# Rotary keys moved into the page rows of a paged latent cache, and split out again by GpSimd

## The chip, the cores and the metric

One core of one Trainium2 chip. The metric is device time in microseconds of one execution. PE is TensorE, PEld its weight loads, DVE is VectorE, ACT is ScalarE, POOL is GpSimd, SP is SyncE. All data is float32 unless said otherwise.

## The reference: what is computed

One layer of a decoder trunk for 512 prompt tokens and 8 sample tokens (one token each for 8 sequences), 520 rows of width 1024. An input projection makes query and key/value latents, a rotary key, a convolution input and two gates. Branch A is a gated depthwise convolution of width 31. Branch B is multi-head latent attention. Then come an output projection, a layer norm, a mixture of 32 experts (two per token) and a gated embedding.

The part at stake is the attention of the 8 sample tokens over a paged cache: 32 pages of 128 past tokens for each of the 8 sequences, 256 pages in all.

```
ckv_past = cache_ckv[layer, page_table]      # (8, 4096, 256)
kr_past  = cache_krope[layer, page_table]    # (8, 4096, 32)
s = (q_lat . ckv_past + q_rope . kr_past) * scale
p = softmax(s);  o = p . ckv_past
```

Every page thus has latents (256 numbers per token) that are used for the scores and again as values, and rotary keys (32 numbers per token) that are used for the scores alone.

## The kernel before, in words

The kernel is one hand-ordered program per engine. Semaphores join them; every instruction's place in its engine's stream is fixed.

**Stage 1** (0 to about 325 us) runs the input projection, the convolution and the gates in `UNITS` (`unit`, `paired`: lines 1019, 1059, 1068 and their neighbours) on PE. Between the units, at places worked out from matmul counts (`K_AT`, `T_AT`, `V_AT`), PE runs the paged attention in 16 steps of 16 pages. For step n there are three pieces: `k_step(n)` makes scores (line 1127: 32 matmuls with the latents; line 1131: 16 with the rotary keys), `k_turn(n)` transposes the probabilities (line 1143), and `v_step(n)` multiplies with the values (line 1157). On PE the order is k_step(0), k_turn(0), v_step(0), k_step(1), and so on, with unit matmuls between all of them.

**Pages.** A page is one DMA of 128 rows of 2048 bytes (`REC` = 512 numbers: two transposed latent chunks of 128, then 256 values) from `in_kv`, and one DMA of 32 rows of 512 bytes from `in_kr`. There are two buffers, chosen by n % 2. SP issues 10 of a step's 16 pages, POOL 6, each with its own semaphores (`s_kv`, `s_kvp`). Page j of a step has b, u = divmod(j, 4); its rotary keys go to partitions 32u to 32u+31 of `krr`, so the four pages of a group b lie below one another on the 128 partitions.

**Order on SP and POOL.** Both run the same loop. `step_keys(n)` loads the page numbers and issues the key DMAs, `step_pages(n)` loads the page numbers and issues the page DMAs:

```
for n in range(2, STEPS):
    pool.wait_ge(s_ks, n - 1)     # k_step(n-2) is done: key buffer free
    step_keys(n)
    pool.wait_ge(s_vs, n - 1)     # v_step(n-2) is done: page buffer free
    step_pages(n)
```

SP has the same, and before step 8 also the four stores of lines 773 to 777. Before `k_step(n)` PE waits for the semaphores of the step's pages and keys. POOL's other work in this stage is four copies of the prompt's rotary keys at its end (line 3015). DVE's stream (`steps`, `some_taps`) has, for each step, the maximum over the scores (`peaks`, line 2125, waits for `k_step(n)`), and between the units the taps of the convolution (line 2118), in order.

**Stages 2 and 3** (from 325 us) are the prompt's attention, the output projections, and the experts with their weight loads (`in_wexp`). The start of each of their transfers hangs on work of PE ahead of it.

Of the kernel before, what the change touches and what calls it, by code (L numbers as in the profile page):

```python
# [33 lines left out]
NPOOL = 5 * NS * NPAGES // 4  # L34
REC = 2 * P + KVL

# [242 lines left out]
A_UKT = A_WUQ + KQ * 2048  # L279
A_KR = A_KV + 2 * STEPS * REC  # L280
A_END1 = A_KR + 2 * 4 * P
assert A_QR + P <= A_OT and A_W1R + 4 * 1024 <= A_XT and A_UKT + 2048 <= A_END1

# [80 lines left out]
def decoder_layer(nc, a, o):  # L364

    ctx = ExitStack()
    with ctx:
# [9 lines left out]
        def at(off, n):  # L377
            return arena[:, off:off + n]
# [42 lines left out]
        kvr = at(A_KV, 2 * STEPS * REC).rearrange("p (s b u n) -> p s b u n", s=2, b=4, u=4)  # L421
        krr = at(A_KR, 2 * 4 * P).rearrange("p (s b n) -> p s b n", s=2, b=4)
        prb = at(A_P, 512).rearrange("p (s n) -> p s n", s=2)
# [281 lines left out]

        def page_keys(n, j):

            b, u = divmod(j, 4)
            return krr[32 * u:32 * u + 32, n % 2, b]

        def narrow(bank, rows, w, ready=None):
# [23 lines left out]
        def _(sp):  # L735
# [21 lines left out]

            def step_keys(n):
                sp.load(numbers, pages[0:1, STEPS * n:STEPS * n + SPN])
                for j in range(SPN):  # L760
                    pg = sp.snap(numbers[j], min_val=0, max_val=NPOOL - 1)
                    sp.dma_start(page_keys(n, j), a["kr"][bass.ds(pg, 1)].rearrange("a p n -> (a p) n")).then_inc(s_kv[n % 2], 16)

            sp.wait_ge(s_con, 112)
            step_pages(0)
            step_keys(0)
            step_keys(1)
            sp.wait_ge(s_q4, 1)
            step_pages(1)
            for n in range(2, STEPS):  # L770
                if n == 8:
                    sp.wait_ge(s_gl, 2 * KC)
                    sp.dma_start(o["conv_p"], ext[:, :, NPR:NPR + CW - 1]).then_inc(s_out, 16)
                    sp.dma_start(o["conv_s"], exs[:]).then_inc(s_out, 16)
                    sp.wait_ge(s_nrm, N_NRM)
                    sp.dma_start(o["ckv"], hT[:, B_CKV:B_CKV + KKV, :]).then_inc(s_out, 16)
                    sp.dma_start(o["krope"], hT[64:96, B_KR, :]).then_inc(s_out, 16)
                sp.wait_ge(s_ks, n - 1)
                step_keys(n)
                sp.wait_ge(s_vs, n - 1)  # L780
                step_pages(n)
# [187 lines left out]
        def _(pe):  # L969
# [145 lines left out]
            def k_step(n):  # L1115
                s, r = n % 2, n // 8
                if n == 0:
                    pe.wait_ge(s_qd, 9)
                elif n >= 2:
                    pe.wait_ge(s_ep, n - 1)  # L1120
                pe.wait_ge(s_kv[s], 32 * SPN * (n // 2 + 1))
                pe.wait_ge(s_kvp[s], 32 * (STEPS - SPN) * (n // 2 + 1))
                bank = 4 + s
                for c in range(KKV):
                    for x in range(SIDES):
                        for bb in range(4):
                            mm(ps[32 * bb:32 * bb + 32, bank, 0:2 * P], qlat[:, c, x, 4 * r + bb, :],  # L1127
                               kvr[:, s, bb, 2 * x:2 * x + 2, c * P:(c + 1) * P], start=(c == 0 and x == 0), stop=False)
                for j in range(2):
                    for bb in range(4):  # L1130
                        y = mm(ps[32 * bb:32 * bb + 32, bank, j * P:(j + 1) * P], qrz[:, j, 4 * r + bb, :], krr[:, s, bb],
                               start=False, stop=(j == 1))
                y.then_inc(s_ks, 1)
# [12 lines left out]
            def v_step(n):  # L1146
                s = n % 2
                pe.wait_ge(s_td2, n + 1)
                if n == 0:
                    pe.wait_ge(s_qa, 3)  # L1150
                    pe.wait_ge(s_qd, 1)
                else:
                    pe.wait_ge(s_oa, n)
                for x in range(SIDES):
                    for u in range(2):
                        for bb in range(4):
                            y = mm(ps[32 * bb:32 * bb + 32, 7, x * KVL:(x + 1) * KVL], pts[:, s, u * P + 32 * bb:u * P + 32 * bb + 32],  # L1157
                                   kvr[:, s, bb, 2 * x + u, 2 * P:REC], start=(u == 0), stop=(u == 1))
                y.then_inc(s_vs, 1)
# [67 lines left out]
            def scores(p, s, x):  # L1227
                hh = 2 * p + x
                if x == 0:
                    pe.wait_ge(s_nout, 2 * p + 2)  # L1230
                    pe.wait_ge(s_kout, 2 * p + 2)
                pe.wait_ge(s_rout, 2 * hh + 2)
                if hh == 0:
                    pe.wait_ge(s_kf, 4)
                    pe.wait_ge(s_cse, 1)
                    pe.wait_ge(s_new, 7)
                else:
                    pe.wait_ge(s_mx, 4 * hh)
                for bank, tiles in ((2, (0, 2)), (3, (1,)), (4, (3,))):
                    for i in tiles:  # L1240
                        c0 = P if i == 2 else 0
                        y = mm(ps[:, bank, c0:c0 + (i + 1) * P], qT[:, p % 4, x, i * P:(i + 1) * P],  # L1242
                               kT[:, s, x, 0:(i + 1) * P], start=True, stop=True)
                    y.then_inc(s_s, 1)
# [1735 lines left out]
        def _(pool):  # L2980
# [11 lines left out]
            def step_keys(n):  # L2992
                pool.load(numbers, pages[0:1, STEPS * n + SPN:STEPS * (n + 1)])
                for j in range(STEPS - SPN):
                    pg = pool.snap(numbers[j], min_val=0, max_val=NPOOL - 1)
                    pool.dma_start(page_keys(n, SPN + j), a["kr"][bass.ds(pg, 1)].rearrange("a p n -> (a p) n")  # L2996
                                   ).then_inc(s_kvp[n % 2], 16)

            pool.wait_ge(s_con, 112)
            step_pages(0)  # L3000
            step_keys(0)
            step_keys(1)
            pool.wait_ge(s_q4, 1)
            step_pages(1)
            for n in range(2, STEPS):
                pool.wait_ge(s_ks, n - 1)
                step_keys(n)
                pool.wait_ge(s_vs, n - 1)
                step_pages(n)

            pool.wait_ge(s_vs, STEPS - 1)
# [128 lines left out]
def laid_out(i):  # L3140
# [19 lines left out]
    def by_pair(w):  # L3160
# [19 lines left out]
    ckT = ckv.transpose(0, 2, 1).reshape(NPOOL, KKV, P, PAGE).transpose(0, 2, 1, 3).reshape(NPOOL, P, KKV * PAGE)  # L3180
    krT = ckr.transpose(0, 2, 1)
    steps = i["page_table"].reshape(2, 4, NPAGES // 4, 4).transpose(0, 2, 1, 3)
# [5 lines left out]
        "w_plg": chunks(i["w_ple_gate"][0]), "w_plp": chunks(i["w_ple_proj"][0]), "plT": chunks(ple.T),  # L3188
        "kv": np.concatenate([ckT, ckv], 2), "kr": krT,
        "state": state, "vec": vec, "con": con, "rope": rope,  # L3190
# [28 lines left out]
```

## Time and profile before

| | us |
|---|---|
| median of 3 runs (range) | 935.86 (932.34 to 937.1) |
| the profiled execution, device time | 934.52 |
| the profiled execution, span of the trace | 932.8 |

Granted TensorE clock 0.99 on average. Read the profile as follows: busy time of each engine first, then the same by stretches of time, then what PE waited for in the stretch with the paged steps, and last the timelines of PE, POOL, SP and DVE around single steps. "issue" as a releaser means that the profile shows nothing that was waited for. Starts are us from the span's start.

### The profile page before, as it was taken

What the parts mean: (1) busy time and instruction counts of PE and PEld (TensorE: products, weight loads), DVE (VectorE), ACT (ScalarE), POOL (GpSimd) and SP (SyncE); (2) the same over time, 40 slices, a digit from 0 to 9 for tenths busy, and PEclk for the clock granted to TensorE, in tenths of its full rate; (3) what the DMA queues carried; (4) which work ended last, traced back from release to release, by engine and by line L of the source; (5) the groups of instructions that cost most, each with busy time, mean ns of one, the idle gap of its engine ahead of it and who ended that gap; (6) DMA issues with size and microseconds to landing.
All of it is one profiled execution on the core that took longest, in us unless ns stands there. A gap on an engine that the chain in (4) does not pass through costs nothing.

```text
span 932.8 us, 14793 instructions
## 1 busy us (share of the span) xinstructions
PE 886.6 (95%) x5217; PEld 533.3 (57%) x5217; DVE 482.7 (52%) x1093; ACT 247.0 (26%) x553; POOL 146.0 (16%) x242
## 2 busy tenths in 40 slices
PE   8999999999999999999999999899999889888897
PEld 7777777777776766656678644443333333333343
DVE  2343789977752258677666346661111211114784
ACT  1122221112243125756620111221111111002246
POOL 0323433334334000000000000011211101111000
PEclk9999999999999999999999999999999989989999
DMA  9977998999999420101241595639999999998601
GB/s 373 372 254 247 337 340 279 332 369 309 320 333 329 169 75 20 49 20 43 113 191 47 212 427 242 237 120 407 425 421 423 424 420 426 422 418 343 236 24 69
DMA packets 76178, 247.61 MB, mean 265 GB/s; under 512 B 15397, under 2 KB 22830, under 8 KB 67110
## 3 DMA queue, kind: packets, MB, share of 16 engines
q1 hardware_dynamic: 54422, 191.42, 53.4%
q0 software_dynamic: 16288, 35.29, 10.6%
q10 hardware_dynamic: 5392, 19.93, 6.0%
q8 instruction: 43, 0.70, 0.3%
q14 instruction: 33, 0.27, 0.1%
HBM read 240.98 MB, written 18.05 MB: 278 GB/s over the span
## 4 chain that ended last, share of the span: by engine, by line
PE 78%; DMA 12%; DVE 5%; issue 2%; ACT 2%; SPq 0%; POOL 0%; DVEq 0%; ACTq 0%; POOLq 0%
PE ps L1068 12%; PE ps L1572 9%; PE ps L1019 8%; DMA arena<-in_wexp 8%; PE ps L1492 6%; PE ps L1594 4%; PE ps L1416 4%; PE ps L1127 3%; PE ps L1157 3%; PE ps L1242 3%; PE ps L1059 3%; PE ps L1697 2%; PE ps L1264 2%; DMA y_scratch<-arena,idy 2%; PE ps L1206 2%
## 5 line engine op out<-in xcount | busy, mean ns | idle before, releaser
L1068 PE MATMUL ps<-arena 128*128 128x260 f32 x544 | 125.9, 387 | 1.4 <-DMA arena<-in_xT 0.9
L1068 PEld LDWEIGHTS ps<-arena 128*128 128x128 f32 x544 | 101.8, 191 | 22.4 <-issue 4.5
L2118 DVE SCALAR_TENSOR_TENSOR arena<-arena,vec 128x512 f32<-128x512 f32 x120 | 81.8, 745 | 0.0
L1019 PE MATMUL ps<-arena 128*128 128x260 f32 x336 | 78.5, 387 | 0.1
L1572 PE MATMUL ps<-arena 128*64 128x512 f32 x288 | 66.8, 617 | 7.4 <-DMA arena<-in_wexp 6.4
L2989 POOL DMA_DIRECT2D arena<-in_kv x96 | 52.3, 546 | 134.7 <-issue 130.9
L2814 DVE TENSOR_TENSOR arena<-ps,arena 128x256 f32<-128x256 f32 x18 | 7.6, 425 | 126.9 <-ACT arena L1967 126.9
L1594 PE MATMUL ps<-arena 128*64 128x512 f32 x288 | 67.4, 610 | 4.2 <-DMA arena<-in_wexp 4.2
L1019 PEld LDWEIGHTS ps<-arena 128*128 128x128 f32 x336 | 62.1, 190 | 12.9 <-issue 3.2
L1572 PE MATMUL ps<-arena,con 128*64 128x512 f32 x288 | 63.8, 595 | 2.3 <-DMA arena<-in_wexp 2.3
L2996 POOL DMA_DIRECT2D arena<-in_kr x96 | 48.2, 502 | 63.8 <-issue 57.2
L1492 PE MATMUL ps<-arena 128*128 128x512 f32 x128 | 58.0, 600 | 0.0
L1594 PEld LDWEIGHTS ps<-arena 128*64 128x64 f32 x288 | 22.1, 141 | 46.6 <-issue 46.6
L1572 PEld LDWEIGHTS ps<-arena 128*64 128x64 f32 x288 | 22.1, 142 | 45.9 <-issue 45.9
L1697 PE MATMUL ps<-arena 128*128 128x512 f32 x96 | 42.5, 596 | 3.0 <-DMA arena<-in_w_plg 1.7
L3042 POOL DMA_INDIRECT y_scratch<-arena,idy x18 | 18.6, 1032 | 171.0 <-PE ps L1557 121.1
L3021 POOL MEMSET peak<- 128x3 f32 x1 | 0.1, 101 | 276.4 <-PE ps L1492 276.4
L1572 PEld LDWEIGHTS ps<-arena,con 128*64 128x64 f32 x288 | 20.3, 137 | 39.4 <-issue 39.4
L1967 ACT ACTIVATE arena<-ps 128x256 f32<-128x256 f32 x18 | 6.9, 385 | 131.1 <-PE ps L1572 131.1
L1242 PE MATMUL ps<-arena 128*128 128x128 f32 (+3 forms) x128 | 38.0, 440 | 0.8 <-DVE arena L2384 0.8
L1127 PE MATMUL ps<-arena 128*32 128x256 f32 x512 | 30.9, 382 | 7.5 <-issue 7.5
L2824 DVE COPY arena<-ps 128x512 f32<-128x512 f32 x17 | 11.8, 692 | 50.8 <-PE ps L1594 50.8
(424 smaller groups left out, 1356.4 us busy)
## 6 DMA issues: line engine op xcount, KB each, us to landing
arena<-in_wexp SPq DMA_DIRECT2D x26, 2048.0 KB, 24.0
arena<-in_kv SPq DMA_DIRECT2D x160, 256.0 KB, 8.8
arena<-in_wexp SPq DMA_DIRECT2D x36, 1024.0 KB, 27.2
arena<-in_kv POOLq DMA_DIRECT2D x96, 256.0 KB, 7.3
arena<-in_w ACTq DMA_DIRECT2D x35, 512.0 KB, 8.4
arena<-in_wexp SPq DMA_DIRECT2D x16, 512.0 KB, 4.7
arena<-in_wo SPq DMA_DIRECT2D x8, 512.0 KB, 4.6
arena<-in_w_out SPq DMA_DIRECT2D x4, 1024.0 KB, 7.3
```

The source lines that it names most:

```text
L1019: y = mm(ps[:, paired_bank(p, n), 0:TH], left(k), right(k), start=(k == 0), stop=(k == KD // 2 - 1))
L1068: y = mm(ps[:, b + h, 0:TH], w[:, k], xT[:, k, h * TH:(h + 1) * TH], start=(k == 0), stop=(k == KD - 1))
L1127: mm(ps[32 * bb:32 * bb + 32, bank, 0:2 * P], qlat[:, c, x, 4 * r + bb, :], kvr[:, s, bb, 2 * x:2 * x + 2, c * P:(c + 1) * P], start=(c == ...
L1242: y = mm(ps[:, bank, c0:c0 + (i + 1) * P], qT[:, p % 4, x, i * P:(i + 1) * P], kT[:, s, x, 0:(i + 1) * P], start=True, stop=True)
L1416: y = mm(ps[:, bank, 0:TH], left(k), right(k), start=(k == 0), stop=(k == KD // 2 - 1))
L1492: y = mm(ps[:, b + h, :], mixT[:, k, t * P:(t + 1) * P], wbig[:, k, h * 512:(h + 1) * 512], start=(k == 0), stop=(k == KD - 1))
L1572: y = mm(ps[64 * x:64 * x + 64, 2, :], turned[:, k, 64 * x:64 * x + 64], wx[slot][:, x, k * 512:(k + 1) * 512], start=(k == 0), stop=(k == ...
L1594: y = mm(ps[64 * x:64 * x + 64, 6 + h, :], htT[:, c, 64 * x:64 * x + 64], wx[slot][:, x, o0:o0 + 512], start=(c == 0), stop=(c == 1))
L1697: y = mm(ps[:, b + h, :], fbT[:, u % 2, k], plg[k][:, h * 512:(h + 1) * 512], start=(k == 0), stop=(k == KD - 1))
L2118: y = v.scalar_tensor_tensor(out=aT[:, c, 0:NPR], in0=win, scalar=wt, in1=aT[:, c, 0:NPR], op0=ALU.mult, op1=ALU.add)
L2989: pool.dma_start(rec[:, n % 2, SPN + j], a["kv"][bass.ds(pg, 1)].rearrange("a p n -> (a p) n")).then_inc(s_kvp[n % 2], 16)
L2996: pool.dma_start(page_keys(n, SPN + j), a["kr"][bass.ds(pg, 1)].rearrange("a p n -> (a p) n")).then_inc(s_kvp[n % 2], 16)
```

## The change

The cache is laid out on the host with the rotary keys inside each page row: 2176 bytes per row (256 latent numbers, 32 key numbers, 256 values). The 128 x 32 keys of a page, which were 32 rows of 128 tokens, now fill 128 partitions: partition 32q + r holds component r of the tokens 32q to 32q+31. The tensor `in_kr` and all its DMAs are gone. POOL's `step_keys(n)` is now four copies of 64 partitions by 256 numbers each (4 groups, 2 pages, 32 tokens), two of which move from the lower half of the partitions to the upper or back; PE waits for them (`s_kf`) ahead of the rotary matmuls of `k_step(n)`. Those write their 128 columns in four runs of 32. The DMA scratch of 4096 bytes per partition makes room for `krr`, which is a tensor of its own now.

```diff
@@ -32,7 +32,7 @@
 ROPEW = KQ * P
 PAGE, NPAGES = 128, 32
 NPOOL = 5 * NS * NPAGES // 4
-REC = 2 * P + KVL
+REC = 2 * P + P // 4 + KVL
 
 
 SIDES, HH = 2, 16
@@ -277,8 +277,7 @@
 A_KV = A_PTS + 1024
 A_WUQ = A_KV + STEPS * REC
 A_UKT = A_WUQ + KQ * 2048
-A_KR = A_KV + 2 * STEPS * REC
-A_END1 = A_KR + 2 * 4 * P
+A_END1 = A_KV + 2 * STEPS * REC
 assert A_QR + P <= A_OT and A_W1R + 4 * 1024 <= A_XT and A_UKT + 2048 <= A_END1
 
 A_PAIR = A_XT
@@ -419,7 +418,7 @@
 
         rec = at(A_KV, 2 * STEPS * REC).rearrange("p (s j n) -> p s j n", s=2, j=STEPS)
         kvr = at(A_KV, 2 * STEPS * REC).rearrange("p (s b u n) -> p s b u n", s=2, b=4, u=4)
-        krr = at(A_KR, 2 * 4 * P).rearrange("p (s b n) -> p s b n", s=2, b=4)
+        krr = sb("krr", [P, 2 * 4 * P])[:].rearrange("p (s b u h i) -> p s b u h i", s=2, b=4, u=2, h=2)
         prb = at(A_P, 512).rearrange("p (s n) -> p s n", s=2)
         pts = at(A_PTS, 512).rearrange("p (s n) -> p s n", s=2)
         swap = at(A_SWAP, P)
@@ -703,11 +702,6 @@
 
         OV_SLOT, OV_LOADS = 0, sum(k % 3 == 0 for k in range(EPAIRS))
 
-        def page_keys(n, j):
-
-            b, u = divmod(j, 4)
-            return krr[32 * u:32 * u + 32, n % 2, b]
-
         def narrow(bank, rows, w, ready=None):
 
 
@@ -755,16 +749,8 @@
                     sp.dma_start(rec[:, n % 2, j], a["kv"][bass.ds(pg, 1)].rearrange("a p n -> (a p) n")
                                  ).then_inc(s_kv[n % 2], 16)
 
-            def step_keys(n):
-                sp.load(numbers, pages[0:1, STEPS * n:STEPS * n + SPN])
-                for j in range(SPN):
-                    pg = sp.snap(numbers[j], min_val=0, max_val=NPOOL - 1)
-                    sp.dma_start(page_keys(n, j), a["kr"][bass.ds(pg, 1)].rearrange("a p n -> (a p) n")).then_inc(s_kv[n % 2], 16)
-
             sp.wait_ge(s_con, 112)
             step_pages(0)
-            step_keys(0)
-            step_keys(1)
             sp.wait_ge(s_q4, 1)
             step_pages(1)
             for n in range(2, STEPS):
@@ -775,8 +761,6 @@
                     sp.wait_ge(s_nrm, N_NRM)
                     sp.dma_start(o["ckv"], hT[:, B_CKV:B_CKV + KKV, :]).then_inc(s_out, 16)
                     sp.dma_start(o["krope"], hT[64:96, B_KR, :]).then_inc(s_out, 16)
-                sp.wait_ge(s_ks, n - 1)
-                step_keys(n)
                 sp.wait_ge(s_vs, n - 1)
                 step_pages(n)
             sp.wait_ge(s_pu, PU[AT["ga", 7]])
@@ -1118,18 +1102,19 @@
                     pe.wait_ge(s_qd, 9)
                 elif n >= 2:
                     pe.wait_ge(s_ep, n - 1)
-                pe.wait_ge(s_kv[s], 32 * SPN * (n // 2 + 1))
-                pe.wait_ge(s_kvp[s], 32 * (STEPS - SPN) * (n // 2 + 1))
+                pe.wait_ge(s_kv[s], 16 * SPN * (n // 2 + 1))
+                pe.wait_ge(s_kvp[s], 16 * (STEPS - SPN) * (n // 2 + 1))
                 bank = 4 + s
                 for c in range(KKV):
                     for x in range(SIDES):
                         for bb in range(4):
                             mm(ps[32 * bb:32 * bb + 32, bank, 0:2 * P], qlat[:, c, x, 4 * r + bb, :],
                                kvr[:, s, bb, 2 * x:2 * x + 2, c * P:(c + 1) * P], start=(c == 0 and x == 0), stop=False)
+                pe.wait_ge(s_kf, 4 * (n + 1))
                 for j in range(2):
                     for bb in range(4):
-                        y = mm(ps[32 * bb:32 * bb + 32, bank, j * P:(j + 1) * P], qrz[:, j, 4 * r + bb, :], krr[:, s, bb],
-                               start=False, stop=(j == 1))
+                        y = mm(ps[32 * bb:32 * bb + 32, bank, 0:2 * P].rearrange("p (u h j i) -> p j u h i", u=2, h=2, j=2)[:, j],
+                               qrz[:, j, 4 * r + bb, :], krr[:, s, bb], start=False, stop=(j == 1))
                 y.then_inc(s_ks, 1)
 
             def k_turn(n):
@@ -1155,7 +1140,7 @@
                     for u in range(2):
                         for bb in range(4):
                             y = mm(ps[32 * bb:32 * bb + 32, 7, x * KVL:(x + 1) * KVL], pts[:, s, u * P + 32 * bb:u * P + 32 * bb + 32],
-                                   kvr[:, s, bb, 2 * x + u, 2 * P:REC], start=(u == 0), stop=(u == 1))
+                                   kvr[:, s, bb, 2 * x + u, 2 * P + 32:REC], start=(u == 0), stop=(u == 1))
                 y.then_inc(s_vs, 1)
 
 
@@ -1231,7 +1216,7 @@
                     pe.wait_ge(s_kout, 2 * p + 2)
                 pe.wait_ge(s_rout, 2 * hh + 2)
                 if hh == 0:
-                    pe.wait_ge(s_kf, 4)
+                    pe.wait_ge(s_kf, 4 * STEPS + 4)
                     pe.wait_ge(s_cse, 1)
                     pe.wait_ge(s_new, 7)
                 else:
@@ -2990,23 +2975,24 @@
                                    ).then_inc(s_kvp[n % 2], 16)
 
             def step_keys(n):
-                pool.load(numbers, pages[0:1, STEPS * n + SPN:STEPS * (n + 1)])
-                for j in range(STEPS - SPN):
-                    pg = pool.snap(numbers[j], min_val=0, max_val=NPOOL - 1)
-                    pool.dma_start(page_keys(n, SPN + j), a["kr"][bass.ds(pg, 1)].rearrange("a p n -> (a p) n")
-                                   ).then_inc(s_kvp[n % 2], 16)
+
+                pool.wait_ge(s_kv[n % 2], 16 * SPN * (n // 2 + 1))
+                pool.wait_ge(s_kvp[n % 2], 16 * (STEPS - SPN) * (n // 2 + 1))
+                for x in range(SIDES):
+                    for h in range(2):
+                        gp.tensor_copy(krr[64 * x:64 * x + 64, n % 2, :, :, h],
+                                       kvr[64 * h:64 * h + 64, n % 2, :, 2 * x:2 * x + 2, 2 * P:2 * P + 32]).then_inc(s_kf, 1)
 
             pool.wait_ge(s_con, 112)
             step_pages(0)
-            step_keys(0)
-            step_keys(1)
             pool.wait_ge(s_q4, 1)
             step_pages(1)
             for n in range(2, STEPS):
-                pool.wait_ge(s_ks, n - 1)
-                step_keys(n)
+                step_keys(n - 2)
                 pool.wait_ge(s_vs, n - 1)
                 step_pages(n)
+            for n in range(STEPS - 2, STEPS):
+                step_keys(n)
 
             pool.wait_ge(s_vs, STEPS - 1)
             pool.wait_ge(s_nrm, N_NRM)
@@ -3178,7 +3164,7 @@
     ple = np.concatenate([i["p_prompt"][0].reshape(NPR, -1), i["p_sample"][0].reshape(NS, -1)])
     ckv, ckr = i["cache_ckv"][0], i["cache_krope"][0]
     ckT = ckv.transpose(0, 2, 1).reshape(NPOOL, KKV, P, PAGE).transpose(0, 2, 1, 3).reshape(NPOOL, P, KKV * PAGE)
-    krT = ckr.transpose(0, 2, 1)
+    krT = ckr.reshape(NPOOL, 4, 32, ROPE).transpose(0, 1, 3, 2).reshape(NPOOL, P, 32)
     steps = i["page_table"].reshape(2, 4, NPAGES // 4, 4).transpose(0, 2, 1, 3)
     out = {
         "xT": chunks(x.T), "x": x, "w1": w1, "wuq": wuq, "ukt": ukt, "wpair": wpair, "wrope": wrope, "wo": blocks(i["w_o_attn"][0]),
@@ -3186,7 +3172,7 @@
         "w_rt": chunks(np.concatenate([i["w_group"][0], i["w_router"][0], np.zeros((D, 28), np.float32)], 1)),
         "wexp": np.concatenate([ex.reshape(NEXP, P, -1), dn.reshape(NEXP, P, -1)], -1),
         "w_plg": chunks(i["w_ple_gate"][0]), "w_plp": chunks(i["w_ple_proj"][0]), "plT": chunks(ple.T),
-        "kv": np.concatenate([ckT, ckv], 2), "kr": krT,
+        "kv": np.concatenate([ckT, krT, ckv], 2),
         "state": state, "vec": vec, "con": con, "rope": rope,
         "lnrows": np.broadcast_to(rows[None], (P, 5, D)), "pages": steps.reshape(1, -1),
         "zeros": np.zeros((P, D), np.float32),
@@ -3202,7 +3188,7 @@
     from concourse.bass_utils import run_bass_kernel_spmd
 
     arrays = laid_out({n: np.asarray(v) for n, v in inputs.items()})
-    nc = bacc.Bacc("TRN2", target_bir_lowering=False, num_devices=1)
+    nc = bacc.Bacc("TRN2", target_bir_lowering=False, num_devices=1, dynamic_dma_scratch_size=4096)
     a = {n: nc.dram_tensor(f"in_{n}", v.shape, mybir.dt.from_np(v.dtype), kind="ExternalInput").ap()
          for n, v in arrays.items()}
     o = {n: nc.dram_tensor(f"out_{n}", s, F32, kind="ExternalOutput").ap() for n, s in OUTS.items()}
```

## Rows read from the trace of the kernel before

**Rows 1.** The page: busy us, share of the span, instructions.
```profile
PE 886.6 (95%) x5217; PEld 533.3 (57%) x5217; DVE 482.7 (52%) x1093; ACT 247.0 (26%) x553; POOL 146.0 (16%) x242
```
**Rows 2.** Windows: stretch, length, busy us by engine, clock, DMA share, GB/s.
```profile
240.00:300.00 60.00, 57.89 (x475) 43.53 (x477) 32.33 (x51) 23.97 (x35) 24.23 (x47) 1.00 0.94 316
330.00:400.00 70.00, 68.64 (x438) 42.49 (x437) 50.49 (x165) 37.02 (x115) 0.00 (x0) 1.00 0.15 48
```
**Rows 3.** Groups of PE, 60 to 325 us: busy, mean ns, idle before.
```profile
L1127 PE MATMUL ps<-arena 128*32 128x256 f32 x512 | 30.9, 382 | 7.5 <-issue 7.5
L1131 PE MATMUL ps<-arena 128*32 128x128 f32 x256 | 10.1, 273 | 0.0
```
**Rows 4.** Timeline of PE: start, length, and idle before.
```profile
72.66 1.93 PE L1157 MATMUL ps<-arena 128*32 128x256 f32 x32
81.73 0.62 PE L1131 MATMUL ps<-arena 128*32 128x128 f32 x16
89.72 1.93 PE L1157 MATMUL ps<-arena 128*32 128x256 f32 x32
97.04 0.62 PE L1131 MATMUL ps<-arena 128*32 128x128 f32 x16
105.31 1.93 PE L1157 MATMUL ps<-arena 128*32 128x256 f32 x32
116.13 0.62 PE L1131 MATMUL ps<-arena 128*32 128x128 f32 x16
156.86 1.93 PE L1157 MATMUL ps<-arena 128*32 128x256 f32 x32
162.56 0.65 PE L1131 MATMUL ps<-arena 128*32 128x128 f32 x16
180.27 1.93 PE L1127 MATMUL ps<-arena 128*32 128x256 f32 x32 [2.31 <-issue]
208.41 1.93 PE L1157 MATMUL ps<-arena 128*32 128x256 f32 x32
215.79 1.93 PE L1127 MATMUL ps<-arena 128*32 128x256 f32 x32 [1.75 <-issue]
217.52 0.65 PE L1131 MATMUL ps<-arena 128*32 128x128 f32 x16
259.63 1.93 PE L1157 MATMUL ps<-arena 128*32 128x256 f32 x32
267.83 0.62 PE L1131 MATMUL ps<-arena 128*32 128x128 f32 x16
```
**Rows 5.** Timeline of POOL.
```profile
93.77 3.51 POOL L2989 DMA_DIRECT2D arena<-in_kv  x6 [5.87 <-issue]
212.46 1.15 POOL L2989 DMA_DIRECT2D arena<-in_kv  x2 [5.87 <-issue]
216.58 2.32 POOL L2989 DMA_DIRECT2D arena<-in_kv  x4 [2.96 <-issue]
311.51 2.29 POOL L3015 COPY arena<-arena 64x512 f32<-64x512 f32 x4 [11.96 <-PE ps L1157]
```
**Rows 6.** Groups of POOL, whole span.
```profile
L3015 POOL COPY arena<-arena 64x512 f32<-64x512 f32 x4 | 2.3, 614 | 12.0 <-PE ps L1157 12.0
L3022 POOL MEMSET arena<- 128x2048 f32 x1 | 1.8, 1801 | 0.0
```
**Rows 7.** Timeline of SP, 160 to 200 us.
```profile
173.90 4.91 SPq L762 DMA_DIRECT2D arena<-in_kr  x10
179.98 8.22 SPq L755 DMA_DIRECT2D arena<-in_kv  x10
```
**Rows 8.** Timeline of DVE around two steps.
```profile
97.72 0.42 DVE L2125 TENSOR_REDUCE peak<-ps 128x1 f32<-128x256 f32 x1 [1.90 <-PE ps L1131]
177.91 2.73 DVE L2118 SCALAR_TENSOR_TENSOR arena<-arena,vec 128x512 f32<-128x512 f32 x4
```
**Rows 9.** DMA issues, 60 to 300 us: count, size, median us to landing.
```profile
arena<-in_kv SPq DMA_DIRECT2D x139, 256.0 KB, 8.7
```

## The prediction

> **What bounds the kernel now.** I read the busy shares of the page first. PE is busy 95% of the span and no other engine more than 57% [rows 1]; the share alone doesn't say that PE sets the time, so I went to the windows. In the paged steps, of which the stretch from 240 to 300 us stands for all, PE is busy 57.9 of 60 us at full clock, and the DMA engines are busy 94% [rows 2]. Both are near their limit, and which of the two decides is seen in what PE waited for. From 60 to 325 us PE idles 7.5 us, all of it ahead of line 1127, at the start of a score step [rows 3]. These are four waits, at steps 7, 8, 9 and 14, of 2.31, 1.28, 1.75 and 2.11 us (the first and the third stand in [rows 4]). No releaser is shown, but the wait there is for pages. So stage 1 is a PE stage in which the pages come just in time: whatever delays PE by a microsecond makes the kernel a microsecond longer, and the most that faster pages can give is 7.5 us. Behind 325 us PE is busy 68.6 of 70 us with hardly any DMA [rows 2], and the transfers of the later stages are started by PE's own progress, so I let a shift of stage 1 pass through whole.
>
> **Part 1: the key DMAs go, page rows grow by 128 bytes.** 256 key DMAs of 16 KB are removed and 256 x 128 x 128 bytes = the same 4.2 MB ride in the rows, so DMA bytes are equal and rows fewer. Pages need 8.7 us from issue to landing in the median [rows 9], and I leave that. On SP the 10 key issues of a step are gone. That matters once: ahead of step 8 the keys went out at 173.90 for 4.91 us and the pages only at 179.98 [rows 7], although v_step(6) had ended at 172.50 by PE's timeline (170.57 + 1.93). The pages of step 8 start some 6 us earlier, those of step 9, pushed by the same delay, some 3 us. By themselves these would end the waits of steps 8 and 9, 3.0 us; with fewer rows in the queues perhaps all 7.5. Bounds of part 1 alone: 0 to -7.5 us. Should the odd row length slow each page by its 6%, the landing grows by 0.5 us and the waits of four steps by 2 us in all; the sum below shows that such a delay is covered.
>
> **Part 2: the copies stand behind page issues that wait for a value step.** POOL's loop is now: copies of step n-2, wait for v_step(n-2), page issues of step n. So the copies of step n come after the page issues of step n+1, and these wait for v_step(n-1). On PE v_step(n-1) is the piece just ahead of k_step(n), whose rotary matmuls (line 1131) now wait for the copies. For steps 1 to 14 there is thus a chain that didn't exist: end of v_step(n-1), POOL wakes and loads page numbers, 6 page issues, 4 copies, line 1131 of k_step(n). Before, the keys had been asked for a whole step earlier. I size the chain, L:
> - End of v_step(1) is 89.72 + 1.93 = 91.65, POOL's first page issue stands at 93.77 [rows 4, 5]: 2.12 us. The load of the page numbers is in it and stays.
> - Six page issues: 3.51 us [rows 5]. The row count per DMA is the same.
> - Four copies. The nearest row is line 3015: 64 x 512, 614 ns each, four in 2.29 us, so one starts every 0.56 us [rows 5, 6]. The new ones have 256 numbers per partition. A memset of 2048 takes 1801 ns, 0.88 ns per number [rows 6]; 256 numbers fewer take off 0.23 us, which gives 3 x 0.33 + 0.39 = 1.4 us. Upper bound 2.3 us, as if nothing were saved (runs of 32 and the move across the halves may cost); lower bound 0.9 us. I take 1.4, between the two rows by length.
> - Hand-over to PE: DVE's line 2125 starts 0.06 us after the end of line 1131 [rows 4, 8]; with a weight load ahead of the matmul I allow 0.35 us.
>
> L = 2.12 + 3.51 + 1.4 + 0.35 = 7.4 us, with bounds of 6.9 and 8.3.
>
> **Against it stands the gap that PE offers**: from the end of v_step(n-1) to the start of line 1131 of k_step(n). From [rows 4]: 97.04 - 91.65 = 5.39 us for step 2, and by the same reading 5.38 to 5.39 for steps 4, 5, 11 and 13; 162.56 - 158.79 = 3.77 for step 6; 81.73 - 74.59 = 7.14 for step 1; 116.13 - 107.24 = 8.89 for step 3, as for step 10; 267.83 - 261.56 = 6.27 for step 12. Where line 1127 had idled, I take the idle time out: 217.52 - 210.34 - 1.75 = 5.43 for step 9, the same for step 14, and 7.18 and 7.19 for steps 7 and 8. New waits at L = 7.4: five times 2.01 (10.0), step 6 3.63, steps 9 and 14 1.97 each (3.9), step 12 1.13, steps 1, 7 and 8 together 0.7, steps 3 and 10 none. Sum 19.5 us. Step 0 has its copies ahead of everything, and step 15's don't wait for a value step.
>
> **What the new waits give back.** The pages of step n are asked for after v_step(n-2), so a wait inside step n-1 gives them more time. Step 7 idled 2.31 and step 6 now waits 3.63; step 14 idled 2.11 and step 13 waits 2.01 with 0.5 us fewer DMA rows' work; steps 8 and 9 have the earlier issues. So all 7.5 us of old idle time goes, once, whichever of the two causes takes it. That is also why a slightly slower page costs nothing. Net: 19.5 - 7.5 = +12.0 us. At L = 6.9 the new waits are 14.3 (net +6.8), at L = 8.3 they are 30.3 (net +22.8).
>
> **Copies beside DVE.** Where the gap is short, DVE stands in front of its own line 2125, which waits for line 1131 (1.90 us idle at 97.72 [rows 8]), so the copies meet an idle DVE. In the long gaps they meet taps: at step 7 POOL would begin its copies at 172.50 + 5.63 = 178.1, in the middle of four taps from 177.91 for 2.73 us [rows 8]. No row shows a copy of POOL beside a tap. Between no effect and four copies that each wait for one tap of 0.7 us, 2.8 us, at the three such steps (3, 7, 10; two of them with 1.5 us to spare), the cost is 0 to 5.6 us; I take 1.0, nearer to nothing, since the taps run out within the window and POOL then goes on alone. The Trainium skill ("SBUF — State Buffer", "Who interferes with whom") says that a VectorE instruction with two inputs in SBUF and a GpSimd instruction that reads SBUF block one another for the whole instruction. By that rule the upper value holds at those steps, and the total is about 4 us more than mine; a reason against this change, but no change of sign.
>
> The other edits: the rotary matmuls write four runs of 32 columns instead of one of 128. They take 273 ns each, 10.1 us in all [rows 3]; I cost the runs at nothing (bounds 0 and, if each took as long as a 256-column one of 382 ns, +1.7 us per 16, of which PE's overlap leaves 0.6 us per step or less). The prompt's key copies of line 3015 move some 5 us later, and the attention of the prompt needs them only after 330 us.
>
> **Sum.** Own run of the profile: 934.5 + 12.0 + 1.0 = 947.5 us. The median of the runs shown is 1.3 us above that run, so a median of about 949 us.
>
> **Rivals.**
> - *The relief is all there is* (faster). Place: line 1127; mechanism: pages without key DMAs land earlier and the four waits go, while the copies stay inside the gaps. Price: -7.5 us, about 928. For the whole price the chain L has to be 5.2 us or less; at 5.5 the new waits are 2.4 us, at 6.0 6.4 us. For it: the 94% of the DMA engines. Against it: 2.12 and 3.51 us are read, and leave no room for copies. Gains and losses are equal at L = 6.1; the kernel is measurably faster below 5.6. Chance 7%.
> - *Both cancel*, within 0.5%: L of 5.6 to 6.6, for instance if POOL's wake-up is shorter when it isn't busy with keys ahead. 931 to 940 us. Chance 7%.
> - *The descriptor space.* POOL's issues ran on without pause but for one stop of 2.96 us after the first two pages of step 10 [rows 5], with no releaser; counting six page and six key DMAs per step this follows the 128th DMA. If it is the end of the descriptor space, a quarter of the space brings it every 32 DMAs: inside the page issues of steps 5 and 10, which stand ahead of the copies of steps 4 and 9. Each adds up to 2.96 us, +5.9, about 955. If every page takes more of it, three times, +8.9, 958. The Trainium skill ("DMA: Bandwidth & Descriptors", "SWDGE vs HWDGE vs iDMA") places the descriptor rings of GpSimd's DMAs in an SBUF carve-out, without a price for a small one. Chance 16%, the blocked copies of the paragraph above included.
> - *Slow copies*: runs of 32 and two copies across the halves at more than 1 us each, L above 9.5 and the new waits above 45 us; 972 and more. Nothing in the profile speaks for it but that no such copy is in it. Chance 8%.
>
> My own case has 62%, with a range of 941 to 957. The range that is to hold 8 times in 10 is 938 to 964: down to where both nearly cancel, up to both mishaps of POOL. About 0.5%, 4.7 us, is what a measurement of this kernel can tell from no change. Faster 7%, same 7%, slower 86%.
>
> **What would show it.** Right: PE idles ahead of line 1131 in twelve of the steps, about 2 us in most, 3 to 4 at step 6, with a copy on POOL as the releaser; ahead of line 1127 it hardly idles; POOL's timeline has six page issues and then four copies with no gap. Span of stage 1 some 12 us longer and everything behind it unchanged. Wrong: no idle time ahead of line 1131 (then the copies are early, and the order isn't what I read), or idle time ahead of line 1127 larger than before (then the pages' rows set the pace), or single copies far from 0.4 us.

## The result, and the profile after

The changed kernel takes 959.5 us (959.25 to 959.78, 4 runs) against 935.4 us: ratio 1.0267, 95% interval 1.0234 to 1.0299, so 24.1 us slower by the medians and 24.7 us by the profiled spans. The forecast was slower, 949 us in a range of 938 to 964. Direction and mechanism held; the loss is nearly twice the 13 us that I had summed, and lies 2.5 us above the 957 with which my own case ended.

From the page of the changed kernel, busy time, against [rows 1]; PE's busy time grew by 5.8 us with the same number of matmuls:

```profile
PE 892.4 (93%) x5217; PEld 534.2 (56%) x5217; DVE 483.7 (51%) x1093; ACT 247.2 (26%) x553; POOL 128.7 (13%) x210
```

Groups of PE up to 340 us, against [rows 3] (line 1111 was line 1127, line 1116 was line 1131). The last column is idle time ahead of the group and what ended it. The waits for pages are gone, and a wait for POOL's copies has come ahead of the rotary matmuls:

```profile
L1111 PE MATMUL ps<-arena 128*32 128x256 f32 x496 | 30.1, 382 | 0.0
L1116 PE MATMUL ps<-krr,arena 128*32 128x128 f32 x240 | 10.1, 288 | 24.7 <-POOL krr L2983 24.7
```

PE's timeline around steps 2, 3, 4, 6, 7, 9 and 10, against [rows 4]; line 1142 is the value step. All 14 steps from 1 to 14 wait. Six of the seven whose gap is 5.4 us (2, 4, 5, 9, 13 and 14) wait 1.92 to 1.94 us, step 6 with its gap of 3.8 us waits 3.69:

```profile
90.84 1.93 PE L1142 MATMUL ps<-arena 128*32 128x256 f32 x32
100.27 0.65 PE L1116 MATMUL ps<-krr,arena 128*32 128x128 f32 x16 [1.93 <-POOL krr L2983]
119.90 0.64 PE L1116 MATMUL ps<-krr,arena 128*32 128x128 f32 x16 [0.32 <-POOL krr L2983]
137.34 0.64 PE L1116 MATMUL ps<-krr,arena 128*32 128x128 f32 x16 [1.93 <-POOL krr L2983]
148.76 1.93 PE L1142 MATMUL ps<-arena 128*32 128x256 f32 x32
175.64 1.08 PE L1116 MATMUL ps<-krr,arena 128*32 128x128 f32 x16 [3.69 <-POOL krr L2983]
185.15 1.93 PE L1142 MATMUL ps<-arena 128*32 128x256 f32 x32
196.77 0.65 PE L1116 MATMUL ps<-krr,arena 128*32 128x128 f32 x16 [2.36 <-POOL krr L2983]
232.27 0.64 PE L1116 MATMUL ps<-krr,arena 128*32 128x128 f32 x16 [1.92 <-POOL krr L2983]
241.97 1.93 PE L1142 MATMUL ps<-arena 128*32 128x256 f32 x32
253.68 0.65 PE L1116 MATMUL ps<-krr,arena 128*32 128x128 f32 x16 [0.70 <-POOL krr L2983]
```

POOL in the same stretches, against [rows 5]. Page issues and then copies, 0.04 us apart:

```profile
94.91 3.51 POOL L2974 DMA_DIRECT2D arena<-in_kv  x6 [12.12 <-issue]
98.46 1.76 POOL L2983 COPY krr<-arena 64x256 f32<-64x256 f32 x4
189.22 2.32 POOL L2974 DMA_DIRECT2D arena<-in_kv  x4 [13.63 <-issue]
192.27 1.15 POOL L2974 DMA_DIRECT2D arena<-in_kv  x2 [0.73 <-issue]
193.46 3.26 POOL L2983 COPY krr<-arena 64x256 f32<-64x256 f32 x4
249.58 4.04 POOL L2983 COPY krr<-arena 64x256 f32<-64x256 f32 x4
```

Read for step 2, the chain is: value step ends 92.77; first page issue 94.91 (2.14 us); six issues 3.51; copies from 98.46 for 1.76; matmul at 100.27. L = 7.50 us, where 7.4 had been worked out.

Windows of the changed kernel (length; busy us of PE, PEld, DVE, ACT, POOL; clock; DMA share; GB/s) show a second thing, in the stretch just behind the wait of step 4. The granted clock there is near the lower of its two levels (1.2 of 2.4 GHz), which no stretch of stage 1 of the kernel before shows (in windows of 1.7 us from 20 to 330 us, none is below 0.9):

```profile
138.20:141.60 3.40, 3.40 (x9) 2.70 (x10) 3.36 (x7) 2.24 (x6) 0.00 (x0) 0.54 1.01 402
60.00:345.00 285.00, 260.31 (x2116) 192.33 (x2115) 170.38 (x301) 67.43 (x117) 78.06 (x150) 0.98 0.81 290
```

and the same stage of the kernel before:

```profile
60.00:325.00 265.00, 257.33 (x2136) 194.83 (x2134) 170.50 (x304) 67.60 (x118) 90.08 (x172) 1.00 0.91 310
```

Value steps and rotary matmuls of the kernel before, for the same steps 4, 6 and 9, and the rotary matmuls of step 15:

```profile
131.43 0.62 PE L1131 MATMUL ps<-arena 128*32 128x128 f32 x16
141.56 1.93 PE L1157 MATMUL ps<-arena 128*32 128x256 f32 x32
170.57 1.93 PE L1157 MATMUL ps<-arena 128*32 128x256 f32 x32
225.53 1.93 PE L1157 MATMUL ps<-arena 128*32 128x256 f32 x32
316.79 0.62 PE L1131 MATMUL ps<-arena 128*32 128x128 f32 x16
```

**Where 24.7 us of span went** (957.5 - 932.8). The rotary matmuls of step 15 start at 340.99 here and at 316.79 before, so 24.2 us of it lie in stage 1:
- Waits: 24.7 us new less 7.5 us old, 17.2.
- Clock: from line 1116 (line 1131 before) to the value step of the same step takes the same time in both kernels, to 0.03 us, where the clock is full; step 4 took 11.42 instead of 10.13 (148.76 - 137.34), steps 6 and 9 took 9.51 and 9.70 instead of 8.01. Three low stretches, 1.3 + 1.5 + 1.7 = 4.5 us. Each stands behind a wait of 1.9 to 3.7 us; other waits of 1.9 us, and those of 2.36 and 2.60 us in steps 7 and 11, had none behind them.
- Restart: in the gap of step 2 there are 100.27 - 92.77 - 1.93 = 5.57 us of work, 5.39 before. The profile lets consecutive groups of matmuls overlap: before, line 1131 starts 1.75 us after line 1127, whose group is given as 1.93 us long. A wait is counted from the end of that group only, so the overlap of 0.18 us is lost beside it. It is 0.14 to 0.19 us in 13 of the 14 steps and 0.05 in step 6; the sum of the three parts puts it at about 2.5 us in all.

### The profile page after: what moved, and what is told of

Its sections match the earlier page's. It is cut to its first block, busy times and chain, and to the rows that moved or that the text cites. A ratio compares the mean times of both kernels' runs of the same rounds, so it can differ in the third digit from the quotient of the medians.

```text
span 957.5 us, 14073 instructions
## 1 busy us (share of the span) xinstructions
PE 892.4 (93%) x5217; PEld 534.2 (56%) x5217; DVE 483.7 (51%) x1093; ACT 247.2 (26%) x553; POOL 128.7 (13%) x210
## 4 chain that ended last, share of the span: by engine, by line
PE 65%; DMA 13%; issue 7%; DVE 6%; POOL 4%; POOLq 3%; ACT 2%; SPq 1%; DVEq 0%; ACTq 0%
DMA arena<-in_wexp 10%; PE ps L1052 9%; PE ps L1557 8%; PE ps L1477 6%; PE ps L1003 5%; PE ps L1401 4%; PE ps L1579 3%; PE ps L1142 3%; PE ps L1227 3%; POOL krr L2983 3%; PE ps L1043 3%; PE ps L1682 2%; POOLq L2971 2%; PE ps L1249 2%; PE ps L1191 2%
## 5 line engine op out<-in xcount | busy, mean ns | idle before, releaser
L1052 PE MATMUL ps<-arena 128*128 128x260 f32 x544 | 127.0, 389 | 1.7 <-DMA arena<-in_xT 1.3
L1052 PEld LDWEIGHTS ps<-arena 128*128 128x128 f32 x544 | 102.8, 192 | 22.9 <-issue 4.5
L1003 PE MATMUL ps<-arena 128*128 128x260 f32 x336 | 79.6, 390 | 0.1
L1003 PEld LDWEIGHTS ps<-arena 128*128 128x128 f32 x336 | 62.9, 192 | 13.4 <-issue 3.8
L1477 PEld LDWEIGHTS ps<-arena 128*128 128x128 f32 x128 | 23.3, 190 | 25.4 <-issue 25.3
L1401 PE MATMUL ps<-arena 128*128 128x260 f32 x168 | 37.0, 382 | 0.0
```

The source lines that it names most:

```text
L1003: y = mm(ps[:, paired_bank(p, n), 0:TH], left(k), right(k), start=(k == 0), stop=(k == KD // 2 - 1))
L1052: y = mm(ps[:, b + h, 0:TH], w[:, k], xT[:, k, h * TH:(h + 1) * TH], start=(k == 0), stop=(k == KD - 1))
L1401: y = mm(ps[:, bank, 0:TH], left(k), right(k), start=(k == 0), stop=(k == KD // 2 - 1))
L1477: y = mm(ps[:, b + h, :], mixT[:, k, t * P:(t + 1) * P], wbig[:, k, h * 512:(h + 1) * 512], start=(k == 0), stop=(k == KD - 1))
```

## The experiments

Theory: the copies' place, behind page issues that wait for a value step, is the whole loss. Rivals: the longer rows or the small scratch cost something of their own; the copies are too slow in any place. Edits are shown shortened. Line numbers are those of the changed kernel, and they move by a few lines where a run's edit adds some. Each ratio is to runs of the kernel before made together with that run.

**Keys of the step before.** All copies and DMAs stay; only what PE waits for changes. The rotary matmuls read older keys, so this one part of the computation differs and the scores are not the right ones. Three added waits on `s_kf` (not shown) keep buffers safe, and the copies of step 15 wait for the value step of step 14.

```diff
-                pe.wait_ge(s_kf, 4 * (n + 1))
+                pe.wait_ge(s_kf, 4 * max(n, 1))
-  ... qrz[:, j, 4 * r + bb, :], krr[:, s, bb], ...
+  ... qrz[:, j, 4 * r + bb, :], krr[:, max(n - 1, 0) % 2, bb], ...
```

> The changed kernel, but the rotary matmuls of step n (n >= 1) read the keys of step n-1 and wait for the copies of step n-1; all copies, page issues and row lengths stay. The computation is thus changed in that one place. Theory (the chain of copies behind the page issues is the whole loss): PE no longer idles ahead of line 1116, the granted clock of stage 1 stays at 1.00, and the time comes back to that of the kernel before or a little under it, 928 to 937 us; what it is under 935.4 is the gain of the missing key DMAs. Rival (2176-byte rows or the small descriptor space cost something of their own): the waits go but the time stays above 942 us, with idle time ahead of line 1111 or longer DMA issues on POOL.

Measured: 931.1 us, ratio to before 0.9977 (0.9957 to 0.9997). Its groups of PE:

```profile
L1112 PE MATMUL ps<-arena 128*32 128x256 f32 x512 | 30.9, 382 | 2.2 <-issue 2.2
L1117 PE MATMUL ps<-krr,arena 128*32 128x128 f32 x256 | 10.0, 273 | 0.0
```

The whole loss goes with the wait, and no stretch of stage 1 is at the low clock any more. The rest of the change is worth about 2 us (0.3 to 4.0): idle time for pages is 2.2 us instead of 7.5, and the rotary matmuls take 273 ns as before, so their runs of 32 columns cost nothing.

**Three pages on POOL.**

```diff
-SPN = 10
+SPN = 13
```

> The changed kernel with SP issuing 13 of a step's pages and POOL 3 instead of 10 and 6. The chain between the value step and the rotary matmuls loses three issues of 0.585 us, 1.75 us, so L goes from 7.5 to about 5.75 us. Theory: the wait in each short step goes from 1.93 to about 0.2 us, step 6 from 3.7 to 2.0, the clock drops mostly go, and the time falls by 17 to 22 us to 938 to 943 us, unless SP's three further issues (1.7 us later) make pages late: then up to 5 us of idle time ahead of line 1111. Rival (waits of PE are not what counts): under 5 us faster than the changed kernel.

Measured: 934.1 us, ratio 1.0004 (0.9981 to 1.0028), 4 us below the range that I expected. The wait of 24.7 us has become:

```profile
L1111 PE MATMUL ps<-arena 128*32 128x256 f32 x512 | 30.9, 382 | 1.2 <-issue 1.2
L1116 PE MATMUL ps<-krr,arena 128*32 128x128 f32 x256 | 10.1, 275 | 3.6 <-POOL krr L2983 3.6
```

SP's three further issues make hardly any page late. What I had missed is that POOL now also loads three page numbers instead of six:

```profile
89.72 1.93 PE L1142 MATMUL ps<-arena 128*32 128x256 f32 x32
93.12 1.73 POOL L2974 DMA_DIRECT2D arena<-in_kv  x3 [12.69 <-issue]
```

From the end of the value step (91.65) to the first page issue it is 1.47 us here, 2.14 with six numbers. L is thus some 0.65 us shorter than I had worked out, about 5.1 us, below the gap of 5.4 us, and step 6 holds 2.65 of the 3.6 us that are left.

**Page numbers loaded ahead of the wait (POOL).**

```diff
             for n in range(2, STEPS):
                 step_keys(n - 2)
+                load_pages(n)
                 pool.wait_ge(s_vs, n - 1)
                 step_pages(n)          # no longer loads the numbers
```

> The changed kernel with POOL's load of the next step's page numbers put ahead of its wait for the value step instead of behind it (1.39 us of the chain). L goes from 7.5 to about 6.1 us. Theory: each short step's wait goes from 1.93 to about 0.5 us, step 6 to 2.3, clock drops at most one or two; the time falls by 15 to 20 us, to 940 to 945 us. Rival (the copies themselves or their contention with VectorE set the wait, so that an earlier start doesn't help): less than 5 us faster.

Measured: 941.7 us, ratio 1.0083 (1.0054 to 1.0111), 9.9 us of waits ahead of line 1116. The time is as expected, and so are 0.51 us of wait in most of the short steps. Step 6 waits 3.10 us and not 2.3, since its copies took 2.60 us; the one stretch at the low clock stands behind it.

**Nine pages on POOL**, the same knob the other way.

```diff
-SPN = 10
+SPN = 7
```

> The changed kernel with SP issuing 7 of a step's pages and POOL 9: the chain gets three page issues longer, 1.75 us, L about 9.3 us. Theory: every one of the 14 steps now waits, the ones that waited 1.93 us wait 3.7, step 6 5.4, steps 3 and 10 0.5 to 2; together 22 to 25 us more, plus one to three further stretches at half clock of 3.4 us: 980 to 990 us. Rival (the wait is set by the landing of pages or by the copies): the time moves by less than 8 us.

Measured: 1008.2 us, ratio 1.0789 (1.0757 to 1.0821): 18 us beyond the upper end of the expectation. Waits of PE, a step with the wait, and the window of stage 1:

```profile
PE ps L1116 <- POOL krr L2983: 55.0, 14, 6.1
```
```profile
304.41 1.08 PE L1116 MATMUL ps<-krr,arena 128*32 128x128 f32 x16 [5.12 <-POOL krr L2983]
```
```profile
60.00:395.00 335.00, 280.05 (x2117) 205.19 (x2116) 170.20 (x301) 67.67 (x117) 98.08 (x196) 0.91 0.69 246
```

The seven steps with the gap of 5.4 us wait 4.4 to 5.1 instead of 3.7 us. Again the load of the page numbers is in it: from the end of the value step of step 12 (337.82 + 1.94 = 339.76) to the first page issue (342.54) it is 2.78 us with nine numbers, against 2.14 with six and 1.47 with three, about 0.22 us per number. In steps 2, 5, 11 and 14, which wait 5.12 to 5.14 us, a stop of POOL of 0.79 us lies in the chain, too. The clock is the larger surprise: 0.91 on average over 335 us. 55.0 - 7.5 = 47.5 us of waits and 14 x 0.18 = 2.5 us of restarts leave 24.6 of the 74.6 us of span to it, and the intervals from line 1116 to the value step, read as above, are 24.1 us longer together. In this run the clock costs about half as much as the waits themselves. The direction, waits that grow with POOL's issues, is the theory's; the size of the clock's part I had again set too low.

**Copies ahead of the wait and the issues.**

```diff
+            step_keys(0)
             for n in range(2, STEPS):
-                step_keys(n - 2)
+                step_keys(n - 1)
                 pool.wait_ge(s_vs, n - 1)
                 step_pages(n)
-            for n in range(STEPS - 2, STEPS):
-                step_keys(n)
+            step_keys(STEPS - 1)
```

> The changed kernel with POOL's order turned: the copies of step n-1 stand ahead of the wait for the value step and the page issues of step n. The copies then hang on the landing of their own pages alone. Theory: PE's waits ahead of line 1116 nearly go; POOL's page issues start when its copies are done, some 3 to 6 us later than now, which costs little since POOL's pages landed earlier than SP's; if a step's last page lands later, PE idles ahead of lines 1111 and 1116. I expect 932 to 942 us. Rival (copies on POOL are too slow in any place, about 2 us plus contention behind the last page): 950 us or more.

Measured: 933.1 us, ratio 1.0004 (0.9982 to 1.0026). Its POOL and its waits of PE:

```profile
94.67 1.76 POOL L2983 COPY krr<-arena 64x256 f32<-64x256 f32 x4 [13.92 <-DMA arena<-in_kv]
96.72 3.51 POOL L2974 DMA_DIRECT2D arena<-in_kv  x6 [0.29 <-issue]
112.30 3.04 POOL L2983 COPY krr<-arena 64x256 f32<-64x256 f32 x1 [12.07 <-DMA arena<-in_kv]
```
```profile
PE ps L1111 <- issue: 2.4, 2, 1.7
PE ps L1116 <- POOL krr L2983: 1.8, 3, 1.3
```

All 64 copies are still in this kernel, in another place, one of them with 3.04 us longer than any in the changed kernel, and the loss is gone: the rival of copies too slow in any place has fallen. POOL's pages are asked for 0 to 7 us later behind the value step than in the kernel before, 3 us on average, and PE idles 2.4 us for pages instead of 7.5.

**The kernel before with the small scratch.**

```diff
-    nc = bacc.Bacc("TRN2", target_bir_lowering=False, num_devices=1)
+    nc = bacc.Bacc("TRN2", target_bir_lowering=False, num_devices=1, dynamic_dma_scratch_size=4096)
```

> The kernel before with the DMA scratch of 4096 bytes and nothing else. Theory: no effect, within 0.4% of the kernel before. Rival (descriptor space): stops of about 3 us between page issues of POOL, of which there was one at 128 DMAs, now every 32; with the keys asked for early these cost little here, up to 5 us, but they show in POOL's timeline.

Measured: 934.0 us, ratio 0.9993 (0.9966 to 1.002). One of its five stops of POOL:

```profile
93.71 1.15 POOL L2989 DMA_DIRECT2D arena<-in_kv  x2 [5.88 <-issue]
95.87 2.33 POOL L2989 DMA_DIRECT2D arena<-in_kv  x4 [1.00 <-issue]
```

The small scratch by itself costs this kernel nothing that can be measured.

**The changed kernel with more scratch.**

```diff
-    nc = bacc.Bacc(..., dynamic_dma_scratch_size=4096)
+    nc = bacc.Bacc(..., dynamic_dma_scratch_size=12288)
```

> The changed kernel with a DMA scratch of 12288 bytes instead of 4096. With 4096, POOL stops for 0.73 us inside the page issues once in every 24 pages (steps 4, 8 and 12), and these stops lie in the chain of steps 3, 7 and 11. Theory: they go, at most one longer stop stays, and the time falls by 1 to 2 us to about 958 us, within the noise. Rival (the small scratch carries a good part of the loss): over 6 us faster.

Measured: 962.1 us, ratio 1.0307 (1.0267 to 1.0347) against 1.0267 (1.0234 to 1.0299), not faster; the 1 to 2 us expected didn't come. The three stops of 0.73 us have gone and one of 2.13 us has come; the waits are 25.4 us, and the clock over the stage is lower:

```profile
60.00:345.00 285.00, 259.51 (x2068) 190.56 (x2070) 169.93 (x299) 66.57 (x114) 78.04 (x149) 0.96 0.82 290
```

The scratch size changes when POOL stops, and the stops are not where the loss is.

**The better version: 13 pages on SP, 3 on POOL, page numbers of both loaded ahead of their waits.** And, to tell the two apart, the kernel before with the numbers of a step loaded once, with its keys.

```diff
-SPN = 10
+SPN = 13
@@ SP and POOL, page loop
+                load_pages(n)
                 wait_ge(s_vs, n - 1)
                 step_pages(n)          # no longer loads the numbers
@@ the kernel before, SP and POOL, step_pages
-                load(numbers, ...)
+                if n < 2:
+                    load(numbers, ...)  # else step_keys(n) has loaded them
```

> The changed kernel with 13 pages on SP and 3 on POOL, and the loads of page numbers of both engines ahead of their waits. The chain is 7.5 - 1.75 - 1.39 = 4.4 us, below every gap but that of step 6 (3.8). Theory: at most 2 us of waits, pages 1.2 to 1.4 us earlier on both queues, no clock drop in stage 1: 926 to 931 us, under the kernel before. Rival (the gain of 13/3 is used up by late pages): 933 to 938 us with idle time ahead of line 1111.

> The kernel before, with the page numbers of a step loaded once, with its keys, on SP and POOL, and not again behind the wait for the value step: pages are asked for 1.2 to 1.4 us earlier. It tells how much of a gain of the run with 3 pages on POOL comes from the early loads alone. Theory: of the 7.5 us of idle time ahead of line 1127, steps 7 to 9 keep a part (stores ahead of step 8), the rest goes: 2 to 5 us faster than the kernel before, 930 to 933 us. Rival (DMA throughput, not the time of asking, sets the landing): same as before.

Measured: 929.9 us, ratio 0.9966 (0.9949 to 0.9984), and 931.5 us, 0.9977 (0.9955 to 0.9998). The first beats both kernels, by 0.3% and 3%; in its stage 1 no idle time is left ahead of the score steps (busy 261.8 of 265 us, 257.3 before):

```profile
92.27 1.73 POOL L2981 DMA_DIRECT2D arena<-in_kv  x3 [13.51 <-PE ps L1147]
94.04 1.77 POOL L2990 COPY krr<-arena 64x256 f32<-64x256 f32 x4
```
```profile
60.00:325.00 265.00, 261.82 (x2184) 195.53 (x2182) 175.24 (x307) 68.72 (x120) 59.50 (x106) 1.00 0.86 309
```

More than half of the gain, 2.1 of 3.7 us, the early loads give to the kernel before as well. The intervals of the two overlap; which share the keys in the rows have in the rest isn't settled.

## Why the prediction was right in direction and short in size

- *PE sets stage 1, and its shift passes through*: right. 24.2 of 24.7 us lie in stage 1, 0.5 behind it.
- *The chain and its length*: right. L = 7.50 us against 7.4. The copies take 398 ns each in the median and start 0.46 us apart, 1.76 instead of 1.4 us for four; the hand-over to PE was 0.05 instead of 0.35 us, and the two misses cancelled, which is luck.
- *New waits of 19.5 us in twelve steps*: the short steps came as worked out (1.93 for 2.01, step 6 3.69 for 3.63), but for step 11 with 2.60. The sum was 24.7 in fourteen, 4.2 more than waits and contention together (20.5).
- *Copies beside DVE, 1.0 us*: mis-sized, with the stops of POOL, at about a fifth. At step 7 the copies took 3.26 us beside three taps, and a stop of 0.73 us stood ahead of them: 2.36 us of wait where 0.2 was forecast. At step 10 they took 4.04 us and used up a gap with 1.5 us to spare. In step 11 a stop of 0.73 us alone made the wait 2.60 us, and steps 1, 8 and 12 waited 0.6 us more than forecast each, with copies of 2.06 to 2.40 us and, in steps 1 and 12, pauses of 0.45 and 0.35 us. An estimate from the rows: with L = 7.50 us in every step and the lost overlap taken off the waits would be 18.8 us; of the 5.9 us above it, about 3.4 are slow copies, 2.2 are POOL's stops and pauses, and 0.3 (step 3) both together. I had argued that the taps run out within the window; at step 10 they do, but the first copy lasts until they have run out:

```profile
249.27 2.73 DVE L2103 SCALAR_TENSOR_TENSOR arena<-arena,vec 128x512 f32<-128x512 f32 x4
```
```profile
L2983 POOL COPY krr<-arena x64: 388/398/2676, 58.9 to 338.3; 64x256 f32<-64x256 f32 x64
```

  Those are DVE at step 10 in its timeline, and the minimum, median and maximum of a copy in ns. The longest copy, from 249.58 for 2.68 us, ends 0.26 us after the four taps, which end at 252.00. The rule that the prediction cites, from the Trainium skill's "SBUF — State Buffer" ("Who interferes with whom"), is that the two instructions contend and that the lock is exclusive. The trace agrees that copies are held up beside taps; that one copy is held up by four taps in a row, while at step 7 each of the four took 0.71 to 0.88 us, is more than a block for one instruction, and no run here shows what decides between the two.
- *Old idle time of 7.5 us goes whole*: right, ahead of line 1111 there is none.
- *The descriptor space*: the first stop of POOL comes the earlier the smaller the scratch, in the kernel before after 128 DMAs as it is and after 44 with 4 KB, in the changed kernel after 85 with 12 KB and after 28 with 4 KB. That fits what it was taken for, but a smaller space brings shorter stops: 2.96 us in the kernel before and 2.13 with 12 KB, 1.00 and 0.73 with 4 KB. The rival's 2.96 us per stop was too much.
- *What was missing*: the granted clock and the restarts, 4.5 and 2.5 us. The prediction treats a microsecond of waiting as a microsecond of time. It is the one term of the sum that I hadn't written down at all. 13.0 + 4.2 + 4.5 + 2.5 + 0.5 = 24.7 us; the 0.5 lies behind stage 1.
- *The range*: that 959.5 lies in 938 to 964 is in part luck. The room above 957 had been left for stops of POOL at 2.96 us each and blocked copies, of which some 6 us came in all; 7 us came from the clock and the restarts, for which neither the sum nor a rival had a place.

## What to carry to other kernels

A copy that replaces a DMA takes on the position of its engine's stream: look for what stands ahead of it there and waits for what, before counting its nanoseconds. When a late wait falls on a PE that had been busy without pause, count more than the wait; here 17 us of it cost 24, and 47 cost 74. The cheap cures were to put the work that hangs on landed data ahead of the wait for a free buffer, and to load registers before a wait and not behind it.

## What the runs showed of the hardware that was not expected

- The granted clock fell to its lower level behind some waits of 1.9 us, within a stage in which PE was busy 260.3 of 285 us and idle hardly anywhere but in these waits, and not behind others of the same length; with nine pages on POOL the rotary matmuls behind the wait took 0.99 to 1.08 us instead of 0.65 in ten of 14 steps. Idle times of up to 2.3 us before the change had no low stretch behind them. The length of the pause alone doesn't decide it, and what does was not tried.
- A copy of GpSimd beside VectorE instructions with two SBUF inputs took 710 to 882 ns at step 7 and up to 2676 ns at step 10 instead of 398, and once 3.04 us with the copies ahead of the issues; VectorE's taps grew to 882 ns at most, from a median of 746.
- On GpSimd the time from the end of the value step to the first page issue grows with the page numbers loaded in it: 1.47, 2.14 and 2.78 us with three, six and nine, and 0.71 us when they are loaded ahead of the wait.
- With a scratch of 4096 bytes GpSimd stopped, after its first stop, once every 24 page DMAs in the changed kernel, every 27 with nine pages a step on POOL, and every 36 page and key DMAs together in the kernel before; what it waits for in a stop no view shows.
